# Moving a mixture-of-experts kernel's combining product into the next pair of experts

## What is computed

```python
logits = (t @ w_router + b_router).astype(jnp.float32)
vals, idx = lax.top_k(logits, TOP_K)                 # 4 of 32 experts for each token
wts = jax.nn.softmax(vals, axis=-1)
comb = jnp.einsum('tk,tke->te', wts, jax.nn.one_hot(idx, N_EXPERTS, dtype=jnp.float32)).astype(u.dtype)
for e in range(N_EXPERTS):
    gu = t @ w_gate_up[e] + b_gate_up[e]             # 1024 -> 2048
    gate = jnp.minimum(gu[:, :D_EXPERT], SWIGLU_LIMIT)
    up = jnp.clip(gu[:, D_EXPERT:], -SWIGLU_LIMIT, SWIGLU_LIMIT)
    h = (up + 1.0) * (gate * jax.nn.sigmoid(SWIGLU_ALPHA * gate))
    out = out + comb[:, e:e + 1] * (h @ w_down[e] + b_down[e])   # 1024 -> 1024
```

## Time and profile before

| what | us |
|---|---|
| median of 3 runs | 1262.28 (1261.79 to 1263.89) |
| the profiled execution | 1262.59 |
| its span in the profile | 1260.5 |
| TensorE busy in the span | 1207.9 |
| VectorE busy | 361.5 |
| ScalarE busy | 223.2 |
| experts' loop on TensorE | about 282 to 1213 |

### The profile page before, as it was taken

One profiled execution on the slowest core, in us unless ns is written; L12 is line 12 of the kernel. 1 busy time (PEld: TensorE's weight loads), 2 busy tenths in 40 slices (PEclk: granted clock), 3 DMA queues, 4 the chain that ended last, 5 costly groups with the idle time before them and its releaser, 6 DMA issues.

```text
span 1260.5 us, 14210 instructions
## 1 busy us (share of the span) xinstructions
PE 1207.9 (96%) x5423; PEld 526.9 (42%) x5423; DVE 361.5 (29%) x830; ACT 223.2 (18%) x405; POOL 28.1 (2%) x62
## 2 busy tenths in 40 slices
PE   7999999999999999999999999999999999999997
PEld 5777777543333333333333333333333333333342
DVE  5463002253313231313223132313132231313233
ACT  2664100143101111110101011101111010101024
POOL 1001004000000000000000000000000000000000
PEclk9999999999999999999999999999999999999999
DMA  9916334338999999999999999999999999999931
GB/s 281 376 69 228 136 134 145 105 150 362 427 429 427 429 428 429 428 428 428 428 428 428 428 429 428 429 428 429 429 428 429 428 429 428 428 428 428 428 155 37
DMA packets 51043, 446.69 MB, mean 354 GB/s; under 512 B 8086, under 2 KB 9206, under 8 KB 26344
## 3 DMA queue, kind: packets, MB, share of 16 engines
q1 hardware_dynamic: 48320, 440.30, 84.0%
q0 software_dynamic: 2592, 6.10, 1.6%
q10 hardware_dynamic: 112, 0.03, 0.0%
HBM read 444.90 MB, written 1.88 MB: 354 GB/s over the span
## 4 chain that ended last, share of the span: by engine, by line
PE 73%; DMA 15%; DVE 5%; issue 3%; ACT 3%; ACTq 0%; POOL 0%; SPq 0%; DVEq 0%; POOLq 0%
PE ps L876 28%; PE ps L635 16%; PE ps L893 14%; DMA ring<-in_w_gate_up 13%; PE ps L944 6%; PE ps L850 3%; PE ps L974 2%; PE ps L862 2%; DVE work L1561 1%; DVE work L1554 1%; DVE work L1558 1%; DMA ring<-in_w_in 1%; ACT work L1174 1%; DMA work<-in_b_down 1%; PE ps L627 1%
## 5 line engine op out<-in xcount | busy, mean ns | idle before, releaser
L876 PE MATMUL ps<-ring,work 128*64 128x512 f32 x2048 | 446.4, 592 | 5.5 <-DMA ring<-in_w_gate_up 5.5
L876 PEld LDWEIGHTS ps<-ring,work 128*64 128x64 f32 x2048 | 145.0, 137 | 288.6 <-issue 268.9
L893 PE MATMUL ps<-ring,gate_a 128*64 128x512 f32 x1024 | 226.0, 594 | 0.0
L635 PE MATMUL ps<-work,ring 128*128 128x288 f32 x752 | 184.3, 406 | 0.1
L635 PEld LDWEIGHTS ps<-work,ring 128*128 128x128 f32 x752 | 142.6, 190 | 39.6 <-issue 0.2
L893 PEld LDWEIGHTS ps<-ring,gate_a 128*64 128x64 f32 x1024 | 71.2, 137 | 133.2 <-issue 128.7
L1554 DVE TENSOR_SCALAR work<-ps 128x512 f32<-128x512 f32 x32 | 22.1, 692 | 354.7 <-PE ps L876 354.7
L1573 DVE TENSOR_TENSOR u_tok<-u_tok,ps 128x512 f32<-128x512 f32 (+1 forms) x96 | 65.7, 684 | 166.8 <-PE ps L944 166.3
L1174 ACT ACTIVATE work<-work 128x512 f32<-128x512 f32 x32 | 20.1, 630 | 489.3 <-DVE work L1554 489.3
L944 PE MATMUL ps<-poolw 128*128 128x512 f32 (+1 forms) x192 | 78.7, 611 | 23.3 <-ACT poolw L1184 23.1
L842 PE MATMUL ps<-x_tok,work 128*64 128x512 f32 x396 | 90.6, 592 | 0.0
(11 more groups left out here) (224 smaller groups left out, 663.4 us busy)
## 6 DMA issues: line engine op xcount, KB each, us to landing
ring<-in_w_gate_up SPq DMA_DIRECT2D x128, 2048.0 KB, 19.6
ring<-in_w_down SPq DMA_DIRECT2D x64, 2048.0 KB, 19.6
ring<-in_w_in SPq DMA_DIRECT2D x7, 2048.0 KB, 12.5
ring<-in_w_proj_b SPq DMA_DIRECT2D x2, 2048.0 KB, 8.4
ring<-in_w_proj_a SPq DMA_DIRECT2D x2, 2048.0 KB, 10.6
ring<-in_w_out SPq DMA_DIRECT2D x2, 2048.0 KB, 8.5
ring<-in_w_ple_gate SPq DMA_DIRECT2D x4, 1024.0 KB, 21.8
ring<-in_w_in SPq DMA_DIRECT2D x2, 1024.0 KB, 12.4
```

Of the source, the lines that this page charges most:

```text
L635: mm = pe.matmul(out(b), lhs, rhs, start=(k == 0), stop=(k == len(pairs) - 1))
L876: mm = pe.matmul(ps[half(g), b, :], xg[:, k, :], whole_piece(q)[:, at + 512 * g:at + 512 * g + 512], start=False, stop=(k == KC - 1))
L893: mm = pe.matmul(ps[half(g), b, :], hT[:, 4 * j + i, :], whole_piece(q)[:, at + 512 * g:at + 512 * g + 512], start=False, stop=(4 * j + i ...
```

## The change

The combining product of pair m - 1 now runs inside pair m, right behind `weigh_gate_up` of its first expert and ahead of `gather`. It has a bank for each of its first four results (4, 5, 6, 7), and the two column halves of the 32-row tile share bank 3, which `sel_w` uses too. VectorE's six additions move with it: they stand behind the hidden values and the bias pick of the first expert, ahead of the copy of hT. The first pair has no pair before it: its product runs all the same, on `o_pair` and `sel_wT` cleared to zero by VectorE, behind the first `gathered(0)`. The product of the last pair stands behind the loop.

```diff
-B_S, B_Y = 3, [4, 5, 6]
+B_S, B_Y = 3, [4, 5, 6, 7, 3]
...
-        def pair_bank(i):
-
-            return B_Y[i % 3], i // 3
+        def pair_bank(t, h):
+
+            return B_Y[2 * t + h] if t < TT - 1 else B_Y[-1]
+
+        def sums_before(bank, m):
+
+            return (m * 2 if bank == B_S else m) + bank_uses[bank]
...
+            def add_pair(m):
+
+                pe.wait_ge(pair_cleared, 2)
+                chunk_read(pe, "out", m * 2 - 1)
+                for t in range(TT):
+                    for h in range(2):
+                        bank = pair_bank(t, h)
+                        pe.wait_ge(emptied[bank], sums_before(bank, m))
+                        mm = pe.matmul(ps[column_half(("y", t, h)), bank, :], sel_wT[:, t, 0:ROWS[t]],
+                                       o_pair[:, 512 * h:512 * h + 512], start=True, stop=True)
+                        if t < TT - 1 or h == 1:
+                            mm.then_inc(filled[bank], 1)
...
                         weigh_gate_up(n)
 
+                        if i == 0:
+                            add_pair(m)
                         gather(n + 1)
...
-                            pe.wait_ge(emptied[B_S], m + bank_uses[B_S])
+                            pe.wait_ge(emptied[B_S], m * 2 + (bank_uses[B_S] + 1))
...
-                    pe.wait_ge(emptied[B_S], m + (bank_uses[B_S] + 1))
-                    chunk_read(pe, "out", n)
-                    for t in range(TT):
-                        for h in range(2):
-                            bank, turn = pair_bank(2 * t + h)
-                            pe.wait_ge(emptied[bank], m * 2 + (bank_uses[bank] + turn))
-                        for h in range(2):
-                            bank, turn = pair_bank(2 * t + h)
-                            pe.matmul(ps[column_half(("y", t, h)), bank, :], sel_wT[:, t, 0:ROWS[t]],
-                                      o_pair[:, 512 * h:512 * h + 512], start=True, stop=True).then_inc(filled[bank], 1)
+            add_pair(passes * PAIRS)
...
+            def add_pair(m):
+
+                for t in range(TT):
+                    for h in range(2):
+                        bank = pair_bank(t, h)
+                        dve.wait_ge(filled[bank], sums_before(bank, m) + 1)
+                        x_half = x2[0:ROWS[t], t, 512 * h:512 * h + 512]
+                        ins = V.tensor_tensor(x_half, x_half, ps[column_half(("y", t, h)), bank, :], ALU.add)
+                        if t < TT - 1 or h == 1:
+                            ins.then_inc(emptied[bank], 1)
+
             dve.wait_ge(gain_landed, 16)
             gathered(0)
+            for t in range(TT):
+                for h in range(2):
+                    wait_filled(dve, ("ple", t, h))
+            V.memset(o_pair, 0.0).then_inc(pair_cleared, 1)
+            V.memset(sel_wT, 0.0).then_inc(pair_cleared, 1)
...
                         pick_expert(pick_gu, e + 1).then_inc(pick_gu_ready, 1)
+                        if i == 0:
+                            add_pair(m)
                         b = chunk_filled(dve, "hT", n)
```

More of the change, by code:

```diff
@@ L346, in hybrid_layer @@
         sel_w_ready = sem("sel_w_ready")
+        pair_cleared = sem("pair_cleared")
         x2_squared = sem("x2_squared")
@@ L954, in _ @@
             for bank in B_Y:
-                pe.wait_ge(emptied[bank], passes * NE + bank_uses[bank])
+                pe.wait_ge(emptied[bank], sums_before(bank, passes * PAIRS) + 1)
             for t in range(TT):
@@ L1176, in _ @@
                         if i == 1:
-                            act.wait_ge(filled[B_S], m + (bank_uses[B_S] + 1))
+                            act.wait_ge(filled[B_S], m * 2 + (bank_uses[B_S] + 2))
                             nc.scalar.copy(sel_wT.rearrange("p t s -> p (t s)"), ps[:, B_S, 0:TT * P]) \
@@ L1187, in _ @@
             for t in range(TT):
[L1188 to L1191, removed]
+                for h in range(2):
+                    bank = pair_bank(t, h)
+                    act.wait_ge(emptied[bank], sums_before(bank, passes * PAIRS) + 1)
                 if t:
```

## The result

| | median us | runs | span in the profile |
|---|---|---|---|
| before | 1262.28 | 7 (1261.37 to 1263.89) | 1260.5 |
| changed | 1266.33 | 7 (1265.27 to 1268.79) | 1264.4 |

The ratio is 1.0031, with a 95% interval of 1.0021 to 1.0040: the change costs 0.31%, about 4 us. The forecast was 1265.8 in a range of 1263.4 to 1267.6.

What follows compares the result with a forecast made beforehand. The weight stream, 58.74 us a pair, was taken to bound the kernel. A stream stop of 2.7 us plus 0.8 for the moved last wait made 3.5 us more: 1266.1 profiled, 1265.8 us as median, range 1263.4 to 1267.6.

Steps and rivals of the forecast that it cites:

- What bounds the kernel: Whole expert loop: the weight stream sets the end, needing 58.74 us a pair against 57.70 for TensorE.
- The rival of a faster stream: Weight stream: it follows TensorE and moves faster when asked, so 24.7 us less, 1237.6 us; chance 0.06.
- TensorE's saving: Each pair: waits of 1.44 and 0.15 us go, 57.70 becomes 56.11 us, worth nothing to the end.
- The cover of VectorE's additions: First experts: the six additions end 1.1 us before the copy of hT begins, so they cost nothing.
- The returning wait: Each pair: a wait replaces the one removed; if 1.44 us long, 6.4 us more, 1268.7 us; chance 0.10.
- The clearing: VectorE behind `gathered(0)`: 0.91 us plus at most as much again, within 3.00 us of idling; costs nothing.
- The gap: Expert 0's down refill: issued later, lead 0.6 us, the stream stops once and is 2.7 us late from there.
- the first refill's row: One of three landing times into an empty queue (7.7, 8.2, 8.8 us); the prediction took 8.2, the down piece's.
- The rival of a warm restart: Expert 0's down refill: stream restarts without its cold start, middle 1263.9 us; chance 0.23.
- The last wait: Last pair: last wait for weights moves to the first expert, with 45.35 us of TensorE work behind it.
- The 0.8 us: Last pair: last down product ends at 1207.3 plus the stream's shift, in place of 1206.5.
- The sum: Whole kernel: 2.7 us for the stream's stop plus 0.8 for the moved last wait, 3.5 us more.

Runs made afterwards that it cites:

- the light kernels: The kernel before and the changed kernel, each loading only half of each down piece from expert 1 on; 1255.77 and 1231.91 us.
- end_none: Kernel before with five banks, first pair written out, one pass through the experts, no product on zeros; 1262.85 us, ratio to before 0.9997.
- the five kernels with a late refill: Changed kernel, first_zero, end_zero, and first_zero with the product on zeros cut to 128 or 256 of 512 columns; 1263.08 to 1266.60 us.
- all three kernels with the full product in expert 0: The changed kernel, first_zero and end_zero; 1266.33, 1266.60 and 1266.50 us.
- first_none: Changed kernel with first pair written out, without the product on zeros and its additions, later products in the new place; 1263.47 us, ratio to before 1.0000.
- after_light: Changed kernel, but from expert 1 on only the first half of each down piece is loaded; 1231.91 us against 1255.77 for the kernel before so halved.
- first_zero: Changed kernel with its first pair written out ahead of the loop, one pass through the experts, product on zeros kept; 1266.60 us, ratio to before 1.0023.
- zero_late: As first_zero, but the whole product on zeros moved from expert 0 to expert 1; 1265.42 us against 1263.35, ratio 1.0012.
- end_zero: As first_zero, but later combining products back behind the second expert, product on zeros kept in expert 0; 1266.50 us, ratio to before 1.0021.

## Why the prediction was right, and where it was off

The mechanism held in both its parts, the stream that stops once and the last wait that moves to the first expert. The sizes in it held less well than the total.

**What bounds the kernel** held: 58.74 us a pair in the changed kernel once it waits (from 519.38 to 578.12), and the light kernels show that it is the weights and nothing else that keep it there. The rival of a faster stream is out, and its size, 24.7 us, is about what the light kernels gave.

**TensorE's saving** was put at 1.59 us a pair and was 1.85. The missing quarter is the product itself: it takes 357.46 - 352.84 = 4.62 us in place of 4.85. Its new place has no part in that. In `end_none` it stands in the old place with the five banks, and takes 397.87 - 393.27 = 4.60. The lines are the old product's first addition and its second tile's weights in the kernel before, then the product in `end_none`:

```profile
336.45 0.69 DVE L1573 TENSOR_TENSOR u_tok<-u_tok,ps 128x512 f32<-128x512 f32 x1 [9.34 <-PE ps L944]
337.26 0.30 PEld L944 LDWEIGHTS ps<-poolw 128*128 128x128 f32 x2 [0.81 <-issue]
...
393.27 4.68 PE L914 MATMUL ps<-poolw 128*128 128x512 f32 x12 [1.35 <-ACT poolw L1197]
```

The second tile uses bank 4 again, which VectorE's first addition empties, and that addition ends at 337.14, just ahead of the tile's weights at 337.26. In `end_none` nothing is held up there. So the 4.85 of the prediction had a short wait for a bank in it; the profile names no releaser, and I read this from the times and the two kernels. The saving was worth nothing, as forecast.

**The cover of VectorE's additions** held. In the changed kernel they run from 299.76 for 3.75 us (4.4 forecast), and VectorE waits 1.61 us before it copies hT:

```profile
299.76 3.75 DVE L1532 TENSOR_TENSOR u_tok<-u_tok,ps 128x512 f32<-128x512 f32 x6
305.12 0.69 DVE L1592 COPY gate_a<-ps 128x512 f32<-128x512 f32 x1 [1.61 <-PE ps L855]
```

I had it free 1.1 us ahead. The returning wait, the second rival, didn't come. The clearing took 0.91 and 0.38 us from 283.03, and VectorE sat idle for another 1.53 us before 285.87: it cost nothing.

**The gap** was the main term: a lead of 0.6 us (0.5 measured), and 2.7 us forecast with bounds of 2.2 to 3.3. Counted at piece 183 it was 3.2 from the first refill's issue, and 3.4 from the landing of the piece ahead. Two terms of it were mis-sized. The first down refill was to land 8.2 us behind its issue into an empty queue: it landed after 7.7, so 2.3 us late and not 2.7. And the second down refill, which the prediction let cost nothing because its lead (4.8 forecast, 317.5 - 313.2 = 4.3 measured) was over 3.9, landed 6.0 us behind the first and not 4.9. The sum had nothing for these 1.1 us. The landing of the first piece after a restart isn't the loss of the stream. What the five kernels with a late refill share is the second landing: 13.6 to 13.8 us behind the first one's issue (here 323.5 - 309.8 = 13.7), which is 8.8 and one transfer of 4.9. So the first refill's row, 8.8, gives 3.4, and is the right one of the three. That a second piece can lag could have been read ahead: behind the one of 8.2 the next, issued at 263.3, landed after 14.7, so 6.8 us behind its forerunner, more than here. The rival of a warm restart falls by this, since in all three kernels with the full product in expert 0 the stream lost 3.2 to 3.7 us. The fixed cost of 2.0 us that the Trainium skill gives (DMA: Bandwidth & Descriptors, "Two cost components") would have made it 1.4; no run with the full product there agrees with that.

**The last wait** moved as forecast. From the quarter at 1165.41 to the end of the last down product it took 45.34 us; the sum had 45.35. That it is so close is in part luck: the product was 0.23 shorter than the sum had it, the quarter (1169.00 - 1165.41 = 3.59 in place of 3.43) and the stretch up to the next bias made up for it. The 0.8 us are there, and `first_none` shows them alone, as 0.7 in the stretch.

**The sum**: 3.2 + 0.8, less 0.1 for the shorter wait ahead of the last product (1.35 for 1.44), is the stretch's 3.87. The first refill came 0.27 us later in this profile, and the part behind the last product's start was 0.24 shorter, 52.30 for 52.54, because the last product is itself 0.25 shorter: 3.90 us of span. Forecast 3.5.

## What to carry to other kernels

Where the loads run at a steady rate, look for two things before moving work: the smallest lead of any load over the landing of the one ahead, because a delay counts only where it brings the lead under what a restart needs (some 3.9 us here); and the last wait for a load, because only the work behind it counts. A placeholder operation that keeps a loop uniform was cheap one expert later and dear at the start of the stream, where the queue is short (0.4 against 3.2 us): if the first turn can't do without it, put it where the lead is long. And a hole in the busiest engine is worth its length only where that engine sets the pace; halving a load shows in one run which it is.

## What the runs showed of the hardware

A queue of weight loads that has run dry doesn't start at full rate: after the issue at 309.8 the rate was 164, 164 and 279 GB/s in the three microseconds from 310, then 459. The first refill shows the same slow start (180, 147 and 295 GB/s in the three microseconds from 287 in the kernel before), with 8.6 to 9.2 us in all profiles from issue to landing of a 2 MB piece that takes 4.9 in the stream.

"3.9 less the lead" is shown for a queue of whole pieces alone. In `after_light`, where the two pieces ahead are half ones, piece 12 is issued at 316.6 with a lead of 1.2 us and lands at 324.1, which is 1.4 us late by the pace of 4.9 and not 2.7. Why the restart is shorter there stays open.

The moment at which the first refill is issued moved by up to 4 us between profiles of kernels that don't differ before it. That is of the size of the effects here, and why the stretches were compared. TensorE's granted clock over the first 60 us doesn't explain it: it was 0.97 both in `first_zero`, with the first refill at 287.12, and in `first_none`, with 290.08. What goes with it is the rate of the loads in those 60 us: 311 and 312 GB/s in `first_none`, `zero_late` and `end_zero` (289.1 to 290.1), 320 to 330 in the others (286.1 to 287.5). Which is cause and which effect stays open.
